# Stores for the recurrence's doubled keys issued from SyncE, VectorE's sums of later shifts one at a time, and GpSimd's chunk-end keys two steps sooner

## The reference

```python
cond = jax.nn.silu(c)
mod = cond @ ada_w[l] + ada_b[l]
sh_m, sc_m, gt_m, sh_f, sc_f, gt_f = jnp.split(mod, N_MOD, axis=-1)
h = rms_norm(x, norm_mix_g[l]) * (1.0 + sc_m) + sh_m
proj = jnp.einsum('bsd,de->bse', h, w_in[l])     # 6688 columns, cut into the inputs of three mixers and the gates
o_a = mixer_diff_attn(a_q, a_k, a_v, ...)        # 4 heads, softmax1 - lam * softmax2
o_b = mixer_hgrn2(b_q, b_ff, b_fb, b_i, b_g, ...)
o_c = mixer_gla(c_q, c_k, c_v, c_g, c_lrf, c_lrb, ...)
merged = g_a * (o_a @ w_up_a[l]) + g_b * (o_b @ w_up_b[l]) + g_c * (o_c @ w_up_c[l])
x = x + gt_m * (merged @ w_out[l])
```

```python
cum = jnp.cumsum(log_a)                          # within a chunk
scores = sum_k q[t,k] * k[s,k] * exp(cum[t,k] - cum[s,k]),  s <= t
o_intra = scores @ v
o_inter = (q * exp(cum)) @ state
state = exp(last) * state + (k * exp(last - cum)).T @ v
```

## Time and profile before

| | us |
|---|---|
| median of 3 runs | 2344.8 |
| lowest and highest of them | 2343.13, 2345.11 |
| the profiled execution | 2341.53 |
| its span in the trace | 2339.6 |

### The profile page before, as it was taken

How to read it: one execution, slowest core, us unless ns; L and a number is a source line. 1 busy time by engine, 2 the same in 40 slices (tenths; PEclk the granted TensorE clock), 3 DMA queues, 4 the chain that set the end, 5 groups by cost and what they waited for, 6 DMA issues and landing times. The chain is left out here.

```text
span 2339.6 us, 28975 instructions
## 1 busy us (share of the span) xinstructions
PE 2271.9 (97%) x11624; PEld 1890.0 (81%) x11624; DVE 1164.6 (50%) x1765; ACT 1000.8 (43%) x1885; POOL 1048.9 (45%) x794
## 2 busy tenths in 40 slices
PE   8899988999999999999999999999999999999998
PEld 4678776777988888888888888888888889888887
DVE  4687887846432122457574334451443345724253
ACT  4665556555533233455553222362332236422224
POOL 2445334445444444532435445544354443544543
PEclk9899999999999999999999999999999999999999
DMA  7222232346232222321213232322222222222221
GB/s 279 88 73 73 109 122 99 133 179 243 91 108 90 98 101 90 108 64 51 73 58 108 94 104 91 108 92 100 79 90 96 95 81 84 97 100 90 99 94 68
DMA packets 42662, 239.79 MB, mean 102 GB/s; under 512 B 5024, under 2 KB 7072, under 8 KB 17184
## 3 DMA queue, kind: packets, MB, share of 16 engines
q1 hardware_dynamic: 39328, 231.23, 28.0%
q10 hardware_dynamic: 3200, 6.71, 0.9%
HBM read 226.38 MB, written 8.39 MB: 100 GB/s over the span
## 5 line engine op out<-in xcount | busy, mean ns | idle before, releaser
L2621 POOL TENSOR_TENSOR WL<-RAW,WH 128x512 fp32r<-128x512 f32 (+1 forms) x688 | 918.0, 1363 | 1148.5 <-ACT WH L1301 1134.1
L731 PE MATMUL PS<-HHI,WH 128*128 128x512 f32 x1488 | 597.9, 402 | 0.3 <-DVE V L1890 0.2
L731 PE MATMUL PS<-HLO,WH 128*128 128x512 f32 x1488 | 582.4, 391 | 0.0
L731 PE MATMUL PS<-HHI,WL 128*128 128x512 f32 x1488 | 582.3, 391 | 0.0
L1301 ACT ACTIVATE WH<-RAW 128x512 fp32r<-128x512 f32 (+1 forms) x688 | 378.5, 613 | 388.2 <-PE PS L731 379.7
L731 PEld LDWEIGHTS PS<-HHI,WH 128*128 128x128 f32 x1488 | 281.3, 189 | 74.5 <-issue 12.3
L731 PEld LDWEIGHTS PS<-HHI,WL 128*128 128x128 f32 x1488 | 281.0, 189 | 60.1
L731 PEld LDWEIGHTS PS<-HLO,WH 128*128 128x128 f32 x1488 | 281.5, 189 | 56.9 <-issue 2.2
L731 PE MATMUL PS<-UF,WH 128*128 128x512 f32 (+1 forms) x832 | 224.0, 357 | 0.0
L1884 DVE TENSOR_TENSOR T<-PS,R 128x512 f32<-128x512 f32 x112 | 76.9, 689 | 212.7 <-PE PS L731 204.8
L731 PEld LDWEIGHTS PS<-UF,WH 128*128 128x128 f32 x832 | 148.3, 189 | 22.8
(11 more groups left out here) (358 smaller groups left out, 3593.5 us busy)
## 6 DMA issues: line engine op xcount, KB each, us to landing
RAW<-in_wts SPq DMA_DIRECT2D x190, 1024.0 KB, 4.8
FW<-in_wts SPq DMA_DIRECT2D x6, 1024.0 KB, 17.3
spill<-T SPq DMA_DIRECT2D x24, 256.0 KB, 3.0
RAW<-in_wts SPq DMA_DIRECT2D x8, 768.0 KB, 4.2
GT<-spill SPq DMA_DIRECT2D x20, 256.0 KB, 5.1
X<-in_xt SPq DMA_DIRECT2D x2, 1024.0 KB, 9.2
out_x<-X SPq DMA_DIRECT2D x8, 256.0 KB, 2.3
X<-in_xt SPq DMA_DIRECT2D x2, 768.0 KB, 8.4
```

The lines of the kernel that those rows point to most:

```text
L731: return e.matmul(o_, l, r, start=start, stop=stop)
L2621: return e.tensor_tensor(o_, a, b, f)
```

## The change

Four things are moved; no arithmetic is added or taken away, and Abs and Exp over PC are made in two halves each.

- SyncE issues the 16 DMAs into QKC. They stand behind the load of unit 10 and ahead of the loads of units 11 and 12.
- ScalarE splits unit 10 before it takes `cqk` out of PSUM, and makes Abs and Exp of the GLA decays right behind the two small exponentials, a half at a time; the Ln and VectorE's part come two rows sooner in the list. On VectorE the sums for the small exponentials go ahead of the copy of `lr`, and the cast of the mask behind it.
- `ada` makes one share at each of the rows 1, 2, 3 and 4, so of four shares two stand a row earlier than before.
- `reach_k` moves from the second substep of level 2 to the third substep of level 1.

```diff
@@ projections
-                for part, row in ((0, 2), (1, 4)):
+                for part, row in enumerate((1, 2, 3, 4)):
                     beside[row].append(("ada", a // 2, a % 2, part))
@@ gate_c
-        for n in range(3):
+        for n in range(1, 3):
             yield [("gate_c", n)]
@@ recurrences
                 elif k == 2:
-                    two.append(("reach_k", r))
                     three.append(("turn", r))
...
+                if k == 1:
+                    three.append(("reach_k", r))
@@ sync_program
-        done = 9
+        done = 10
+        load(done)
+        for m in range(2):
+            q.wait_ge(*at(("ev", U["cqk", 0], m)))
+            for n in range(8):
+                r, c = 64 * (n // 2 % 2) + 32 * (n % 2), 32 * (n // 2)
+                t = e.dma_start(QKC[r:r + 32, n // 4, m, :], T0[m][c:c + 32, :])
+                t.then_inc(*up(f"dupc{m}", *([("qc", m)] if n == 7 else []), by=16))
@@ scalar_program
+        split_after(U["lr", 0])
         for m in range(2):
             q.wait_ge(*at(("t", i, m)))
             q.wait_ge(*at(("h", "mix", 4 + m)))
             e.activation(T0[m][:, :], PS[:, BANK[i, m], :], ACT.Copy, ...)
-            if m == 0:
-                split_after(U["lr", 0])
-        for m in range(2):
-            q.wait_ge(*at(("ev", i, m)))
-            for n in range(8):
-                r, c = 64 * (n // 2 % 2) + 32 * (n % 2), 32 * (n // 2)
-                t = e.dma_start(QKC[r:r + 32, n // 4, m, :], T0[m][c:c + 32, :])
-                t.then_inc(*up(f"dupc{m}", *([("qc", m)] if n == 7 else []), by=16))
...
+        for p in range(2):
+            q.wait_ge(*at(("zc_ev", p)))
+            e.activation(G3[0][:, p, :], PC[:, p, :], ACT.Abs).then_inc(*up("a_mix", ("abs_c", p)))
+        for p in range(2):
+            q.wait_ge(*at(("abs_c", p)))
+            e.activation(G3[0][:, p, :], G3[0][:, p, :], ACT.Exp, scale=-1.0).then_inc(*up("a_mix", ("exp_c", p)))
@@ vector_program: ada, one share to a call
-            for kk in (2 * part, 2 * part + 1):
```

## The result

| | before | changed |
|---|---|---|
| median of five runs, us | 2344.67 | 2333.08 |
| lowest and highest, us | 2342.78, 2345.11 | 2330.7, 2334.37 |
| the profiled execution, us | 2341.53 | 2334.37 |
| its span, us | 2339.6 | 2332.6 |

The ratio is 0.9951, with a 95% interval of 0.994 to 0.9963: 11.6 us faster, of which the interval allows 9 to 14. A second set of five runs of the changed kernel, beside other runs of before, gave 2334.12 against 2345.09 and 0.995 (0.9938 to 0.9962); 11 to 12 us faster were expected of it. The forecast was 5.9 us faster, so the sign and the range were right and the size was half of what was measured. The two profiled executions differ by 7.2 us only: that of before was lower than its median by 3 us, that of the changed kernel 1.3 above its own.

A forecast was written before the change was run, and what follows sets the result against it. TensorE, busy 97% of the span, bounds the kernel, so only its idle or lower-clock time can be won. Start 1.3, keys 1.3 + 2.1, shares 0.75 + 1.8 - 1.35 sum to 5.9: 2344.8 - 5.9 = 2338.9 us, range 2332.0 to 2347.5.

The forecast's parts named there:

- The sum: Whole kernel: 1.3 + 1.3 + 2.1 + 0.75 + 1.8 - 1.35 = 5.9 us gained, median 2338.9; chance 0.46.
- Rival C: Faster: SyncE issues copies in 0.47 us, part 1 gives 4.0, some half-clock time spared; 10.6 us, about 2334; chance 0.14.
- Rival B: TensorE's next waits, behind VectorE and ScalarE, take the gains; 1 to 3 us left, 2342.8; chance 0.27.
- Part 1: Start: copies on SyncE bring the Ln and the `scale` ending TensorE's 7.35 us wait sooner; gain 1.3 us.
- 64.1 + 16p: End of the Ln in us behind unit 11's load, p being SyncE's pitch per copy; 74.3 at p = 0.64.
- 7.35 us for part 1: Upper bound of part 1's gain if the load of unit 11 doesn't bind: TensorE's whole wait ending at 87.30.
- Part 2: `reach_k` two steps sooner: KH ahead of WL pieces on GpSimd; 1.3 us at first run, 2.1 at TensorE's KH waits.
- the first run: First run of the recurrence: KH and G sooner on GpSimd, ZB's sum shortened before the 111.94 wait; gain 1.3 us.
- the two waits for KH: TensorE's waits at about 301 us (2.5, gaining 0.45) and 437.56 (1.64, gaining 1.65 in all); together 2.1 us.
- Part 3: One share at each of four rows on VectorE: gains 0.75 and 1.8 us at SCT waits, loss 1.35 elsewhere.
- rival D: Slower: shares ahead of `collect` cost TensorE 1.7 us at seven places, net 7.2 lost, 2352; 0.13 with the slow pitch.
- Rival E: SyncE issues copies no sooner because unit 10's load ahead waits for WH of unit 8; given no chance of its own.

The follow-up runs named there:

- the four pairs: Pairs among the eight kernels with every choice of start, shares and keys, differing in one part only; averages by ratios: start 2.2, shares 4.0, keys 6.1 us.
- the start only: Kernel before with only the copies on SyncE and the new ScalarE and VectorE order; shares in pairs, keys at old step: 2342.48 us, 0.9994.
- the changed kernel without the shares or without the keys: Two kernels from the changed one: shares in pairs again, 2333.09 us, 0.9958; `reach_k` back at its old step, 2336.13 us, 0.9967.
- the two experiments with the loads: Changed kernel with load of unit 11 ahead of the 16 copies, 2327.96 us; then also load of unit 12 between the two groups of eight, 2324.68 us.
- the start alone: With both loads moved: kernel before plus the start's changes, load 11 ahead of the copies, load 12 between their groups; shares and keys as before: 2334.06 us, 0.9951.
- the keys alone: Kernel before with only GpSimd's chunk-end keys (`reach_k`) two steps sooner: 2337.81 us, 0.9971.
- the three pairs beside the keys' move: Kernels with `reach_k` moved, shares one by one against in pairs: with the start changed, with it undone, and with both loads moved (0.9918 against 0.9919).

## Why the prediction was right or wrong

**The sum.** Sign and range were right; 5.9 us were forecast and 11.6 measured. As a forecast of idle time, which is all that it reckoned, 5.9 was right in total: the same work has 6.5 and 5.5 us less of it. Term by term that was in part luck. On average over the four pairs the start took 0.9 us of idle time where 1.3 was booked, the keys 2.8 where 3.4 was booked, and the shares 3.0 where 1.2 was booked. In time the three gave 2.2, 6.1 and 4.0 us by the ratios, so every term was too small, the keys' and the shares' by some 3 us each.

What the sum lacked has two parts. One is the clock: none in total in the first profile of the changed kernel, 2.4 us in the second. The other is the step from the profiled execution to the median. "3 us lie between them whatever the kernel" was wrong: the changed kernel's two profiled executions took 2334.37 and 2332.63, 1.3 above its median and 1.5 below the second one. Forecast for a profiled execution were 2335.6, off by 1.2 and 3.0; for the median 2338.9, off by 5.8. So 2 to 4 of these 5.8 us are that the profile of before came from an execution 2 to 3.6 us faster than that kernel's medians. In part such differences go with the clock. Of the 50 other executions of before that have a granted clock on record, the nine at 0.990 or less took 2346.5 us on average and the fourteen at 0.993 or more 2343.2. But the profiled one stands at 0.992 and is faster than all ten others at 0.992, 2341.8 to 2344.6. Why it is stays open.

**Rival C** said 2334, which came out. One of its two reasons is wrong: SyncE doesn't issue the copies in 0.47 us. The other, some 2 us of time at the lower clock spared, is a gain that the forecast didn't have and that the runs show: 0.1 and 2.4 us of busy time in the two profiles. **Rival B** said 2342.8, which the interval excludes, but what it describes happens at single places: at 129 us a faster TensorE only waits longer, and of the wait at 437 us half comes back.

**Part 1, the copies on SyncE: near in size, by another route.** The formula stood: the Ln was to end at 64.1 + 16p. The copies took 11.63 us, so p = 0.727, which gives 75.8 against a measured 76.31. In the four other traces with the same start (the changed kernel again, the start only, and the changed kernel without the shares or without the keys) they took 10.7 to 11.0 us, so p was 0.67 to 0.73. The mis-sized term is p, taken as 0.64 from the typical issue and not from the mean of the same 16 copies on ScalarE, 0.72, which the prediction had named and passed over. The copies in the changed kernel by tile, their issue in ns (min, median, max), show why:

```profile
L674 SPq DMA_DIRECT2D QKC<-T x16: 590/590/1943, 55.8 to 66.8; - x16
```

The median is 0.59 and the longest 1.94 us: a few long ones make the mean, and the mean counts for what stands behind sixteen. So the Ln came 0.6 us later in this trace, and 0.3 to 0.6 sooner in the four others, counted from the first copy; never 1.3. The product that was to gain 1.3 began 0.63 later here. TensorE waits 3.56 + 2.62 = 6.2 us in two pieces instead of 7.35 in one and 1.2 in three small ones for WL, and the sixteen products behind the wait, which in the kernel before read

```profile
87.30 3.09 PE L731 MATMUL PS<-DD 64*128 64x128 f32 x16 [7.35 <-DVE DD L1884]
```

take 1.97 us instead of 3.09. In the kernel before, the granted clock during them was 0.50. But that gain isn't sure either: in the second profile of the changed kernel they take 3.09 us again, behind a wait as short as in the first.

```profile
87.48 3.09 PE L739 MATMUL PS<-DD 64*128 64x128 f32 x16 [2.64 <-DVE DD L1885]
```

What the start is worth is therefore read from the timed runs, 2.2 us on average, good to 2.

The Trainium skill ("DMA: Bandwidth & Descriptors", section "Issuing engines are not separate DMA queues") says that another engine saves only the issuing sequencer's time. The trace agrees: ScalarE's 9.05 us of issue are gone, and a copy costs SyncE on average 0.67 to 0.73 us, where it cost ScalarE 0.72.

That the load of unit 11 would bind was right, and it is the main thing in this case: the two experiments with the loads took some 8 us more, 8.4 by the medians and 7.7 by the ratios. The bound that stood for its absence, 7.35 us for part 1, was too small. With both loads moved the start alone gave 11 us. In its profile 7.5 us are idle time, about as bounded, and 5.5 are busy time.

**Part 2, the keys.** At the first run 1.3 us were booked. In the changed kernel, GpSimd, VectorE and TensorE, beside the earlier trace rows:

```profile
98.35 1.75 POOL L2622 TENSOR_TENSOR KH<-KH,QKC 128x512 f32<-128x512 f32 x1
...
104.85 2.85 POOL L2622 TENSOR_TENSOR G<-G,G 128x1024 f32<-128x1024 f32 x1
...
105.36 3.43 DVE L1891 SCALAR_TENSOR_TENSOR QKB<-ZB,G 128x1024 f32<-128x1024 f32 x1
108.82 1.23 DVE L1891 SCALAR_TENSOR_TENSOR ZB<-ZB,G 128x1024 f32<-128x1024 f32 x1
...
110.82 1.34 PE L739 MATMUL PS<-DD 64*128 64x128 f32 x13 [1.56 <-DVE SCT L2208]
```

KH starts at 98.35, and G at 104.85 instead of 106.71. G now meets the sum into QKB, which takes 3.43 us instead of 2.31, and leaves ZB, which takes 1.23 instead of 3.29. The wait of 2.51 became 1.56: 0.95 against 1.3. The prediction saw ZB's time come down and not that another sum would pay for G.

For the two waits for KH 2.1 us were booked. At 301 us the step "the next product of TensorE waits for a `scale` that isn't sooner, so 0.45 remains" failed. The `scale` is indeed hardly sooner, but no product waits for it: it ended at 300.26 before and ends at 299.29 with the keys alone, and TensorE asks at 300.0. What holds it then is the `collect`, by 0.68 us. So 1.1 us was kept there alone, 1.8 with the shares. At 437 us 1.65 were booked; the wait went whole, 1.7 us, and 0.9 came back in a wait of 0.80 for SB at 434.17 of the changed kernel. Together about 2 to 3 us: rival B's mechanism, at part of its price. So the waits were booked about right, and yet the keys alone gave 5.9, of which the traces place 3.2 in the busy time. That kind of gain had no term in the sum; only rival C had one.

**Part 3, the shares.** 1.2 us were booked, and the idle time fell by 1.4 to 5.5. The gain was undersized, by rows that were read one wait at a time; at 262 and 467 us TensorE gained 1.6 and 1.5 us where 0.45 each was booked. The timed runs gave 3.7 by the medians alone, and 0.2 to 3.3 by the ratios in the three pairs beside the keys' move. Of rival D, the places with a share ahead of a `collect` cost what was said or less: the wait of 1.99 grew by 0.42 (0.75 booked), at 423 us one of 0.39 is new (0.6 booked). D is out.

**Rival E**, the load of unit 10 ahead of the copies, cost nothing: the copies start at 55.78 on SyncE, and started at 55.76 on ScalarE.

## What to carry to other kernels

When DMAs are moved to another engine's queue, list what stands behind them in that queue and who waits for it; here the order of two loads around 16 copies decided some 8 us with nothing else altered. For a row of DMAs with something waiting behind, take the mean of their issues, not the median.

Where the bounding engine's clock moves, compare the same work in two traces and split it into idle and busy time: an edit can win one and lose the other, and the sum of waits then tells neither. Then look whether the two were only exchanged: between two waits that another engine ends, a busy time 1.5 us shorter made a wait 1.5 us longer, and the 17.8 us stayed. One profile is one execution, so take what a part is worth from timed runs, best from several pairs that differ in it alone.

## What the runs showed of the hardware

- The same 16 copies of 32 partitions x 512 numbers, SBUF to SBUF, took 11.4 to 12.6 us of issue on ScalarE in five traces and 10.7 to 11.6 on SyncE in six. Before and in the changed kernel the longest took 2.6 and 3.3 times the median.
- The same products of TensorE (some 2514 rows) took from 443.5 to 452.2 us of busy time in fourteen profiles. The extremes have a granted clock of 0.99 and 0.96; the fewest idle us (23.2) did not go with the least busy time.
- Sixteen small products behind TensorE's wait took 3.09 us at a granted clock of 0.50 before. In two profiles of the changed kernel, behind 2.62 and 2.64 us of waiting, they took 1.97 us in one and 3.09 in the other.
- A VectorE sum over 128x1024 took 1.23 us alone and 3.29 to 3.43 beside a GpSimd product of the same size. Moving GpSimd's product moved part of the price to another sum: the two sums took 5.60 us before and 4.66 after.
